# Norm seams of a two-block network: last units paired, norm steps reordered, unread products taken out

## What is computed

```python
# first block
for l in range(2):
    h = h + 0.5 * _swiglu(_rmsnorm(h, ffn1_norm[l]), ...)       # 1024 -> 2816 -> 1024
    h = h + _hybrid_mixer(_rmsnorm(h, mix_norm[l]), ...)
    h = h + 0.5 * _swiglu(_rmsnorm(h, ffn2_norm[l]), ...)
h = _rmsnorm(h, final_norm)
# second block
h = _layer_norm(h, ln_in_g, ln_in_b)
for l in range(2):
    h = _layer_norm(ALPHA * h + _mixer(h, ...), ln1_g[l], ln1_b[l])
    h = _layer_norm(ALPHA * h + _peer(h, ...), ln2_g[l], ln2_b[l])
```

## Time and profile before

| | us |
|---|---|
| median of 3 runs | 2994.54 |
| lowest and highest run | 2993.27, 2996.62 |
| the profiled execution, its own time | 2994.6 |
| its span, first to last instruction | 2992.8 |
| PE busy | 2942.8 (98%) |
| DVE, ACT, POOL busy | 2127.1, 1495.4, 703.0 |
| mean granted clock of TensorE | 0.997 |

### The profile page before, as it was taken

How to read it: one execution, slowest core, us unless ns; L and a number is a source line. 1 busy time by engine, 2 the same in 40 slices (tenths; PEclk the granted TensorE clock), 3 DMA queues, 4 the chain that set the end, 5 groups by cost and what they waited for, 6 DMA issues and landing times.

```text
span 2992.8 us, 54764 instructions
## 1 busy us (share of the span) xinstructions
PE 2942.8 (98%) x18492; PEld 2623.8 (88%) x18492; DVE 2127.1 (71%) x3622; ACT 1495.4 (50%) x2390; POOL 703.0 (23%) x455
## 2 busy tenths in 40 slices
PE   8999999999999999999999999999999999999998
PEld 7889888888888888899999978888899999978887
DVE  6667566766766667758986667777758996767776
ACT  4455444444654445445555545545545455544544
POOL 0001300000031002117777400000207877600000
PEclk9999999999999999999999999999999999999999
DMA  6544655555454554457888777776446887777775
GB/s 221 189 159 137 200 168 187 170 188 185 152 181 157 185 187 151 155 173 205 198 210 187 195 247 241 241 241 199 162 162 193 195 212 197 178 247 242 240 242 189
DMA packets 255982, 581.52 MB, mean 194 GB/s; under 512 B 61336, under 2 KB 127168, under 8 KB 255344
## 3 DMA queue, kind: packets, MB, share of 16 engines
q1 hardware_dynamic: 210656, 547.94, 56.7%
q0 software_dynamic: 45200, 31.93, 6.8%
HBM read 542.92 MB, written 36.84 MB: 194 GB/s over the span
## 4 chain that ended last, share of the span: by engine, by line
PE 84%; DVE 9%; ACT 3%; issue 2%; DMA 1%; POOL 1%; SPq 0%; ACTq 0%; DVEq 0%
PE acc L785 32%; PE work L721 26%; PE work L731 9%; PE work L733 5%; DVE wsp L447 3%; PE acc L849 3%; PE acc L1187 2%; ACT wsp L444 2%; PE acc L1324 1%; PE work L986 1%; PE work L1000 1%; ACT scratch L1403 1%; PE work L1109 0%; DMA back<-second_dram 0%; POOL st L574 0%
## 5 line engine op out<-in xcount | busy, mean ns | idle before, releaser
L447 DVE TENSOR_TENSOR wsp<-ring,wsp 128x1024 fp32r<-128x1024 f32 x908 | 1105.3, 1225 | 559.2 <-ACT wsp L444 555.0
L444 ACT ACTIVATE wsp<-ring 128x1024 fp32r<-128x1024 f32 x944 | 984.9, 1052 | 506.1 <-PE work L721 213.2
L721 PE MATMUL work<-xsp,wsp 128*128 128x256 f32 x7872 | 971.6, 285 | 6.0 <-DVE wsp L447 3.2
L785 PE MATMUL acc<-wsp,hsp 128*128 128x512 f32 x4128 | 957.7, 391 | 8.9 <-DVE hsp L2593 7.1
L721 PEld LDWEIGHTS work<-xsp,wsp 128*128 128x128 f32 x7872 | 953.8, 192 | 10.9 <-DVE wsp L447 4.5
L785 PEld LDWEIGHTS acc<-wsp,hsp 128*128 128x128 f32 x4128 | 770.3, 188 | 173.2 <-issue 8.8
L731 PE MATMUL work<-xsp,wsp 128*128 128x512 f32 x1408 | 502.9, 400 | 7.2 <-DVE xsp L1821 5.7
L689 POOL DMA_INDIRECT second_dram<-rows_sb,spots x256 | 470.4, 1838 | 146.6 <-issue 87.5
L733 PE MATMUL work<-xsp,wsp 128*128 128x256 f32 x1408 | 395.7, 281 | 0.0
L574 POOL TENSOR_TENSOR st<-st,mhalf 128x1 f32<-128x1 f32 x24 | 20.6, 864 | 1562.7 <-DVE st L1841 805.5
L731 PEld LDWEIGHTS work<-xsp,wsp 128*128 128x128 f32 x1408 | 265.3, 188 | 74.3 <-DVE xsp L1821 6.8
(11 more groups left out here) (346 smaller groups left out, 2206.2 us busy)
## 6 DMA issues: line engine op xcount, KB each, us to landing
ring<-in_stream SPq DMA_DIRECT2D x944, 512.0 KB
back<-second_dram SPq DMA_DIRECT2D x256, 128.0 KB, 3.1
second_dram<-back POOLq DMA_DIRECT2D x32, 512.0 KB, 14.6
second_dram<-arena SPq DMA_DIRECT2D x184, 64.0 KB
rows_sb<-in_rows POOLq DMA_DIRECT2D x10, 512.0 KB, 6.1
second_dram<-acts SPq DMA_DIRECT2D x72, 64.0 KB
second_dram<-rows_sb,spots POOLq DMA_INDIRECT x256
h_saved_dram<-h POOLq DMA_DIRECT2D x2, 1024.0 KB, 5.0
```

The lines of the kernel that those rows point to most:

```text
L444: self.eng.activation(dst[:, 0, :], src, ACT.Copy).then_inc(high_done, 1)
L447: self.eng.tensor_tensor(dst[:, 1, :], src, dst[:, 0, :].bitcast(F32), ALU.subtract)\
L721: mm = pe.matmul(out_, lhsT=w[:, a, 128 * c:128 * c + 128], rhs=xsp[:, b, c, :], start=(c == 0 and n == 0), stop=(c == DC - 1 and n == 2))
L785: mm = pe.matmul(ACC[2 * b + n][:, :], lhsT=act[:, pa, 128 * b:128 * b + 128], rhs=w[:, pw, 512 * n:512 * n + 512], start=(first and m == ...
```

## The change

It does five things.

- No unread products: `busy` is 0 at every seam and the six between the blocks are gone, so PE waits.
- A new `last_units` takes the last two units of the mixers and of the peer together: block 0 of both, then block 1 of both. It waits for both units' low parts first, and in the peer for the activations of both.
- The layer norm's steps on DVE are reordered. The gain step of block 0 (`centred`) goes to y in place of h and stands before the adds of block 1; block 1's last step is written in two halves of 512, and PE waits for each half (`ln_half`) before four transposes.
- `split.upto` of the next part's second unit moves behind `x_lows` on DVE (mixers and peer), and on ACT between the squares of block 0 and of block 1.
- The small `w16` parts of the first block's mixer are made ahead of the adds and squares of the seam; the `iota2` copy moves into the first mixer of the second block.

```diff
@@ norm_xT
                 if between is not None:
                     acc_claim(pe, between)
-                    for _ in range(6):
-                        pe.matmul(ACC[0][:, :], lhsT=xsp[:, 0, 6, 0:128], ...)
                 for c in range(DC):
                     if c == 0:
                         pe.wait_ge(ev(second[0]), second[1])
-                    elif c == DC // 2 and second[0] == "xs_ready":
+                    elif c == DC // 2:
                         pe.wait_ge(ev(second[0]), second[1] + 1)
@@ tensor
+            def last_units(G, i, acts):
+                ws = [G.unit(pe, i, 0), G.unit(pe, i + 1, 0)]
+                for b in range(NB):
+                    for u in range(2):
+                        order = [(m, n) for n in range(2) for m in range(3)] if u else [(m, n) for m in range(3) for n in range(2)]
+                        for m, n in order:
+                            pa, pw = PARTS[m]
+                            mm = pe.matmul(ACC[2 * b + n][:, :], lhsT=acts[u][:, pa, 128 * b:128 * b + 128],
+                                           rhs=ws[u][:, pw, 512 * n:512 * n + 512], start=False, stop=(u == 1 and m == 2))
+                            if u and m == 2 and n == 0:
+                                mm.then_inc(ev("half_block"), 1)
+                        if b:
+                            mm.then_inc(unit_done, 1)
+                        elif u:
+                            mm.then_inc(ev("first_block"), 1)
@@ ffn, mix1 (the same in both)
-                X = norm_xT(part, xs, (...), (...), 9 if n > 1 else 0)
+                X = norm_xT(part, xs, (...), (...), 0)
@@ mix2, peer
-                X = norm_xT(part, h, ("ln_first", 2 * l + 1), ("ln_ready", 2 * l + 1), 20 if l else 41, part)
+                X = norm_xT(part, h, ("ln_first", 2 * l + 1), ("ln_half", 4 * l + 1), 0, part)
-                X = norm_xT(part, h, ("ln_first", 2 * l + 2), ("ln_ready", 2 * l + 2), 20, part + "s")
+                X = norm_xT(part, h, ("ln_first", 2 * l + 2), ("ln_half", 4 * l + 3), 0, part + "s")
@@ peer, end of V
-                for q in range(122, 128):
-                    value_unit(q, False, q == 127)
+                for q in range(122, 126):
+                    value_unit(q, False, False)
+                pe.wait_ge(act_low, TILES + NKEYS * (l + 1))
+                last_units(G, 126, (hsp[:, 0, :, :], hsp[:, 1, :, :]))
@@ scalar, ln_squares (squares likewise)
                 for b in range(NB):
+                    if b and ahead is not None:
+                        split.upto(ahead)
                     act.wait_ge(ev("mean_ready"), NB * normed[0] + b + 1)
@@ scalar, mix1
-                squares(f"ffn1{l}")
                 act.wait_ge(const_in, 48)
                 act.activation(w16[:, 0, :], pr1[:, l, P_W16:P_W16 + 128], ACT.Copy).then_inc(ev("w16_high"), 1)
+                squares(f"ffn1{l}")
@@ vector, ffn end
                 split.upto(G.u + 3 * FT)
+                if part[0:4] == "ffn1":
+                    dve.wait_ge(const_in, 48)
+                    dve.wait_ge(ev("w16_high"), l + 1)
+                    tt(w16[:, 1, :], pr1[:, l, P_W16:P_W16 + 128], w16[:, 0, :].bitcast(F32), ALU.subtract)...
                 add_to_h(part, (G, 3 * FT - 1), 0.5, 1.0)
@@ vector, layer_norm (new order)
+                if part is not None:
+                    add_half(0, 0, last, 1.0, ALPHA, True)
+                    add_half(0, 1, last, 1.0, ALPHA, True)
+                mean(0)
                 dve.wait_ge(rows_in, 32 * (n + 1))
+                step(centred(0, whole))
+                if part is not None:
+                    add_half(1, 0, last, 1.0, ALPHA, True)
+                    variance(0)
+                    add_half(1, 1, last, 1.0, ALPHA, True)
+                else:
+                    variance(0)
+                mean(1)
...
+                scaled()
+                ins = normal(0, whole)
...
+                variance(1)
+                step(centred(1, whole))
+                scaled()
+                for s in halves_:
+                    ins = normal(1, s)
+                    if n < 3 * DEPTH:
+                        ins.then_inc(ev("ln_half"), 1)
@@ vector, mix2 and peer
-                split.upto(Group(part, "tt").u + 1)
```

More of the change, by code:

```diff
@@ L1388, in head_squares, with squares @@
                     ins.then_inc(ev("head_sums"), 1)
-            def squares(before=None):
+            def squares(before=None, ahead=None):
                 for b in range(NB):
+                    if b and ahead is not None:
+                        split.upto(ahead)
                     for n in range(2):
@@ L1406, in _, with ln_squares @@
             normed = [0]
-            def ln_squares():
+            def ln_squares(ahead=None):
                 for b in range(NB):
+                    if b and ahead is not None:
+                        split.upto(ahead)
                     act.wait_ge(ev("mean_ready"), NB * normed[0] + b + 1)
@@ L1416, in ffn @@
             def ffn(part, l, gain, before, tiles):
-                squares(before)
+                squares(before, Group(part, "ffn").u + 1 if before is not None and before[0:3] == "mix" else None)
                 split.upto(Group(part, "ffn").u)
@@ L1642, in mix1 @@
                 xsp_highs(part, "yT1", pr1[:, l, P_Y:P_Y + 8], 4, 4)
-                split.upto(Group(part, "wout1").u + 5)
+                split.upto(Group(part, "wout1").u + 4)
             def mix2(part, l):
@@ L1695, in mix2 @@
                 xsp_highs(part, "yT1", yg[:, l, :], 4, 4)
-                split.upto(Group(part, "wout").u + DC + 1)
-                ln_squares()
+                split.upto(Group(part, "wout").u + DC)
+                ln_squares(Group(part, "wout").u + DC + 1)
             def peer(part, l):
@@ L1779, in peer @@
                     split.upto(G.u + j + 1)
[L1780 to L1781 removed]
+                ln_squares(G.u + 129)
             yg = pr2[:, :, Q_GAIN:Q_GAIN + 8]
@@ L1855, in rms @@
                 if part[0:3] == "mix":
[L1856 to L1861, removed]
+                    x_lows(part, gain)
+                    split.upto(Group(part, "ttk").u + 1)
+                    return
+                split.upto(Group(part, "ffn").u + 1)
                 if part == "ffn10":
@@ L2217, in layer_norm, with mean @@
                 normed[0] += 1
-                for b in range(NB):
+                def mean(b):
                     if part is None:
@@ L2242, in variance, with centred @@
                         .then_inc(ev("square_ready"), 1)
-                variance(0)
-                dve.wait_ge(ev("mean_ready"), NB * normed[0])
-                dve.wait_ge(rows_in, 32 * (n + 1))
-                for b in range(NB):
-                    hb = h[:, b, :]
-                    step(stt(hb, hb, moments[:, b, 0:1], rows[:, 0:1024], ALU.add, ALU.mult))
-                    if b == 0:
-                        variance(1)
-                    asked[0] += 1
-                    dve.wait_ge(ev("rsqrt_ready"), asked[0])
-                    ins = stt(hb, hb, moments[:, b, 1:2], rows[:, 1024:2048], ALU.mult, ALU.add)
-                    if b == 0 and n < 3 * DEPTH:
-                        ins.then_inc(ev("ln_first"), 1)
-                    if n == 3 * DEPTH:
-                        ins.then_inc(ev("out_ready"), 1)
+                def centred(b, s):
+                    dve.wait_ge(ev("mean_ready"), NB * (normed[0] - 1) + b + 1)
+                    return stt(y[:, b, s], h[:, b, s], moments[:, b, 0:1], rows[:, s], ALU.add, ALU.mult)
@@ new lines, in normal @@
+                def normal(b, s):
+                    return stt(h[:, b, s], y[:, b, s], moments[:, b, 1:2], rows[:, 1024 + s.start:1024 + s.stop],
+                               ALU.mult, ALU.add)
+                whole, halves_ = slice(0, 1024), (slice(0, 512), slice(512, 1024))
+                if part is not None:
+                    add_half(0, 0, last, 1.0, ALPHA, True)
+                    add_half(0, 1, last, 1.0, ALPHA, True)
+                mean(0)
+                dve.wait_ge(rows_in, 32 * (n + 1))
```

76 lines of the change are left out of this document (45 added, 31 removed).

## The result

| | us | against the kernel before on the same chip |
|---|---|---|
| before | 2994.18 (2993.24 to 2998.55) | |
| after | 3005.58 (3004.81 to 3007.67) | 1.0033 [1.0024, 1.0043], +11.4 us |
| after, the profiled execution | 3004.92, span 3003.1, mean clock 0.991 | |

A forecast was written before the change was run, and what follows sets the result against it. PE, busy 98% of the span, was taken to bound the kernel. From 2994.6 us, -1.4 without the clock, +6.8 at layer norm seams and +6.7 at rms seams gave 3006.7, stated as 3006.5; range 2997 to 3016.

The forecast's parts named there:

- Rivals 2 and 3: 2: every seam falls and stays low into the products, 3019.2, chance 0.10; 3: x_lows wait hides low clock, 2993.2, 0.05.
- Rival 4: In the four mixers the pair waits for the second unit's low part, 1.2 us each: 3011.5 us, chance 0.05.
- Layer norm seams: All four with products behind them fall to low clock, 1.6 us each, plus 0.2 twice for slow transposes: +6.8 us.
- Rms seams: Each of five falls to low clock with chance 2 in 3, costing 2.0 us: +6.7 us.
- Rival 1: Clock holds at the five rms seams, so not slower: 3000.0 us, within 0.2%; chance 0.20.
- The order at mixer to peer: At two seams DVE's new layer norm order readies block 1 for PE 1.4 us earlier: -2.8 us together.
- wa: Ahead of two mixers POOL issues this load later, delaying first products 0.3 us (ffn21 to mix20) and 0.6 (peer0 to mix21): +0.9.
- The end: Program end: the peer's paired units stall PE 1.2 us, the new order wins back 0.8: +0.4 us.
- w16: First block's mixers: its low part goes ahead of the adds in two seams, mostly given back: +0.1 us for both.
- The forecast's sum without the clock: Mixer to peer order -2.8, wa +0.9, the end +0.4, w16 +0.1: -1.4 us.

The follow-up runs named there:

- products_back: Changed kernel with unread products put back at all nine seams and between layer norm blocks, everything else kept: 2996.86 us, 1.0003 against the kernel before.
- products_back_rms: Changed kernel with 9 unread products put back at the five rms seams alone: 3000.52 us, 1.0018 against the kernel before.
- changed_again: The changed kernel run once more, unedited, for a second trace: 3003.61 us, one execution.
- products_out_alone: Kernel before with all 146 + 24 unread products taken out and nothing else changed: 3004.35 us, 1.0030 against the kernel before.
- old_norm_order: products_back with DVE's layer norm steps in the order of the kernel before, pairs and halves kept: 2998.87 us, 1.0006 against the kernel before.
- before_again: The kernel before run once more, unedited, for a second trace: 2998.56 us, one execution.

## Why the prediction was right

**What decides: right.** The loss is the clock behind the seams; the rest sums to about nothing (products_back). Rivals 2 and 3 are out. Rival 4 is out as well: the mixers' pair starts without a stall (1265.01, no idle ahead of it). That the total came within 0.9 us is partly luck: by the medians the clock was put 3.0 us too high and everything else 2.4 us too low, and the two errors nearly cancel.

**Layer norm seams, forecast 4 x 1.6 + 2 x 0.2 = 6.8.** After less products_back: D 1.55, E1 1.92, F 1.60, E2 1.89, together 6.96; in products_back_rms 6.97. In changed_again and products_out_alone (against before) it is 4.67 and 4.58, as some of these seams cost little or nothing there. The mean of the four is 5.8. One picture behind the price was wrong: the low stretches in after are 6.7 us or longer, not 3.4. The price comes out near the same because most of the first 3 us goes to transposes and waits: at E1 the next products run at half rate from 1278.46 to 1282.2 only, 3.7 us, and half of that is 1.9 us.

**Rms seams, forecast 5 x 2/3 x 2.0 = 6.7: the mis-sized term.** In three executions without products, 8 of 15 seams fell (2, 2 and 4 of 5). Less the late load they cost 0.39 to 2.09 us, 1.2 on average, which is 3.3 us for each execution. The price was too high, since it took every fall to reach into the products. In three of the eight it did: the clock stayed at 0.50 for 6.8 us, and the cost was 1.94 to 2.09, as priced. In the other five it stayed low for 3.4 us and was back by the time the products started or within about 0.8 us of that; these cost 0.4 to 1.0, for the late transposes alone or nearly so. So it was at mix10 to ffn20 in after, where the first wide product takes 0.50 us again:

```profile
391.58 1.94 PE L750 MATMUL work<-cst,scratch 128*128 128x128 f32 x8 [2.29 <-DVE scratch L1879]
393.31 1.75 PE L758 MATMUL work<-cst,scratch 128*128 128x128 f32 x8
395.78 0.50 PE L731 MATMUL work<-xsp,wsp 128*128 128x512 f32 x1 [0.72 <-DVE xsp L1846]
```

The break behind the transposes shrank from 1.22 us to 0.72 here and to 0.82 at ffn20 to ffn11, which took back some of their lateness. The chance of 2 in 3 cannot be told from 8 in 15 with so few seams, and the traced executions are not typical: that of after had the highest mean clock of its six runs (0.991 against 0.988 to 0.990), that of products_out_alone the lowest of its seven. Rival 1 was thus half true: about half of these seams held. What decides at a given seam is open. It is not the length of the idle time alone: 2.88 us held at 202 and 2.59 us fell at 584 in after, and the same seam of the same kernel with the same 2.59 us held in changed_again.

Traces give the clock 5.8 + 3.3 = 9.1 us against 13.5 forecast, and the medians 10.5. (The medians' own split, 6.8 for the rms seams and 3.7 for the others, is not sharper than 4 us.)

**The order at mixer to peer, forecast -1.4 each: -1.37 and -1.36.** The turned block 1 starts 5.48 us behind the last product, forecast 5.4. One step of the working failed without harm. It had POOL's first serve held by the add, to 0.4 us behind it; the serve took 0.57 and was through 0.06 us behind the add (1271.90, 1271.84). The 0.34 us went into gaps of 0.1 to 0.2 us between DVE's later steps. Of the gain, 0.93 us is the order (old_norm_order); the rest is the pair and the halves.

**wa, forecast +0.3 at D and +0.6 at F: +0.11 and +0.67.** In products_back the load goes out 2.36 us later than before at F, counted from the weight copy ahead of the seam; the forecast had 2.3. Moving it takes 0.89 and 0.91 off, so the late load was the cause of all of it.

**The end, forecast +0.4 (1.2 of stall less 0.8 of order): +0.56.** With the pair in place the parts measure 1.33 and 0.74. They do not add freely: without the pair the end is +0.59 as well, so there the new order costs time where the forecast had it win 0.8, and the stall is no cost that can be had back by itself. What can is POOL's held serve, 0.39 us.

**w16, forecast +0.1:** the rms seams of the kernels with their clock up sum to 0.08 to 0.26, where before_again has 0.07.

**What stays open.** The forecast's sum without the clock was -1.4; the seams say -1.28, the median +0.95 with an interval of about 2.7 us to either side. The trace of products_back has 4.73 us between the seams, 3.0 of them inside the two peers, where before_again shows changes of the same size. It was not followed further.

## What to carry to other kernels

Unread products that end before their engine is needed cost under 0.1 us at the rms seams here and were worth 0.4 to 2.1 us where the clock would have fallen: take such work out only after looking at what the granted clock does behind the gap, in several executions, since the same gap fell in one and held in the next. When a norm's steps are reordered, follow the small requests to the slow engine too: here a load queued behind a serve cost 0.9 us at each of two seams, and one held serve 0.4 us at every norm. Compare the same instruction on both sides of a place: between two executions of the kernel before that repeated within 0.07 us where whole times moved by 4.

## What was not expected of the hardware

- **Which DVE step holds POOL.** A serve that began during the gain step, whose two tensors are in SBUF, took 1.53 us, or 1.00 when the step was cut in half. One that began during an add took 0.57 us, and that step has its second input in PSUM. Both hold within 0.02 us at all four later layer norms (E1, F, E2, the end) of after. The Trainium skill (SBUF — State Buffer, Who interferes with whom) has the same: a DVE instruction with two SBUF inputs contends with a GpSimd instruction that reads SBUF, one with at most a single SBUF input does not, outside what the page calls the 2-port perf modes. The forecast had taken both for holding. A single SBUF input alone does not free POOL: at the rms seams of after a serve that began in the 128x512 scale step (L1879, one SBUF tensor and a scale for each row) took 0.74 to 0.76 us against 0.55 to 0.57 with no DVE step running, and ended 0.43 us behind that step. Whether that is the page's exception, no run here tells.
- **Transposes keep the clock up.** With fifteen unread 128x128 transposes in 1.80 us it stayed at 1.00 over all five rms seams, as with nine products in 2.20 us; with neither it fell at 8 of 15.
